# A two-block transformer kernel: 96 of 512 tokens of the expert stage taken out of the dense products and computed from fetched rows

## The reference

```python
def one_block(hx):                                   # 128 tokens
    q = (hx @ w_q).reshape(TOKEN_BLOCK, PEER_HEADS, 2, PEER_HALF)
    s = jnp.einsum('nhpd,hpkd->nhpk', q, sub_keys).astype(jnp.float32)
    top_s, top_i = lax.top_k(s, PEER_TOPK)
    ...                                              # best 16 of the 16 x 16 sums, for 8 heads
    expert = (i1 * N_KEYS + i2).reshape(TOKEN_BLOCK, PEER_HEADS * PEER_TOPK)
    gate = jax.nn.softmax(best_s, axis=-1).reshape(TOKEN_BLOCK, PEER_HEADS * PEER_TOPK)
    act = jax.nn.gelu(jnp.einsum('nd,ned->ne', hx, u[expert]), approximate=False)
    return jnp.einsum('ne,ned->nd', gate * act, v[expert])
```

## Time and profile before

| | us |
|---|---|
| median of 3 runs | 2600.27 (2599.69 to 2601.42) |
| the profiled execution, whole | 2599.47 |
| its span, first to last instruction | 2597.4 |
| TensorE busy | 2467.7 |
| POOL busy | 1556.1 |
| VectorE busy | 1379.4 |
| ScalarE busy | 594.9 |
| mean granted TensorE clock | 0.981 |

### The profile page before, as it was taken

How to read it: one execution, slowest core, us unless ns; L and a number is a source line. 1 busy time by engine, 2 the same in 40 slices (tenths; PEclk the granted TensorE clock), 3 DMA queues, 4 the chain that set the end, 5 groups by cost and what they waited for, 6 DMA issues and landing times. The chain is left out here.

```text
span 2597.4 us, 37806 instructions
## 1 busy us (share of the span) xinstructions
PE 2467.7 (95%) x12856; PEld 1258.9 (48%) x12856; DVE 1379.4 (53%) x2401; ACT 594.9 (23%) x1238; POOL 1556.1 (60%) x1048
## 2 busy tenths in 40 slices
PE   6979989999999999989999999999899898999997
PEld 3435534444555555434444444444357544457743
DVE  6695748999677777129722222240204533554434
ACT  2313211111222222111111111110216332245412
POOL 6763459888776676799866666660570067830063
PEclk8989999999999999999999999999999899999999
DMA  6324443555457857877755656560220022310021
GB/s 262 104 73 162 143 149 125 155 150 153 135 154 240 253 157 237 266 258 265 243 203 201 205 199 207 198 217 17 82 98 1 9 82 94 101 49 1 9 73 49
DMA packets 189246, 375.31 MB, mean 144 GB/s; under 512 B 13664, under 2 KB 79200, under 8 KB 189152
## 3 DMA queue, kind: packets, MB, share of 16 engines
q1 hardware_dynamic: 119696, 332.54, 38.3%
q10 hardware_dynamic: 69456, 41.50, 5.4%
HBM read 302.68 MB, written 71.30 MB: 144 GB/s over the span
## 5 line engine op out<-in xcount | busy, mean ns | idle before, releaser
L687 PE MATMUL ps<-hT,parts 128*128 128x512 f16 x4800 | 1057.3, 381 | 38.1 <-DVE arena L1397 14.5
L636 POOL TENSOR_SCALAR parts<-ring 128x1024 f16<-128x1024 f32 x261 | 289.3, 1108 | 806.7 <-PE ps L687 781.2
L687 PEld LDWEIGHTS ps<-hT,parts 128*128 128x128 f16 x4800 | 467.2, 98 | 599.2 <-issue 23.4
L687 PE MATMUL ps<-arena 128*128 128x512 f16 x3072 | 668.7, 381 | 6.8 <-DVE arena L1738 6.8
L639 POOL TENSOR_TENSOR parts<-ring,parts 128x1024 f16<-128x1024 f32 x261 | 566.6, 2171 | 21.8
L687 PEld LDWEIGHTS ps<-arena 128*128 128x128 f16 x3072 | 301.5, 98 | 374.9 <-issue 16.8
L1733 DVE TENSOR_TENSOR arena<-arena 128x512 f32<-128x512 f32 x128 | 142.3, 1112 | 438.2 <-DMA arena<-gate_mem 435.2
L657 POOL TENSOR_TENSOR arena<-ring,arena 128x1024 f16<-128x1024 f32 x128 | 283.2, 2213 | 10.6
L637 POOL TENSOR_SCALAR ring<-ring 128x1024 f32<-128x1024 f32 x261 | 281.0, 1077 | 0.0
L655 POOL TENSOR_SCALAR arena<-ring 128x1024 f16<-128x1024 f32 x128 | 147.6, 1153 | 171.6 <-PE ps L687 171.6
L1228 ACT ACTIVATE spare<-ps 128x512 f32<-128x512 f32 x128 | 76.5, 597 | 567.5 <-PE ps L687 421.2
(11 more groups left out here) (171 smaller groups left out, 2257.5 us busy)
## 6 DMA issues: line engine op xcount, KB each, us to landing
ring<-w SPq DMA_DIRECT2D x133, 512.0 KB, 3.3
ring<-u SPq DMA_DIRECT2D x128, 512.0 KB, 3.9
ring<-v SPq DMA_DIRECT2D x128, 512.0 KB, 3.4
act_mem<-spare SPq DMA_DIRECT2D x128, 256.0 KB, 4.0
gate_mem<-arena ACTq DMA_DIRECT2D x4, 8192.0 KB, 43.0
arena<-act_mem SPq DMA_DIRECT2D x128, 256.0 KB, 3.6
arena<-gate_mem SPq DMA_DIRECT2D x128, 256.0 KB, 3.8
arena<-ada_w SPq DMA_DIRECT2D x48, 512.0 KB, 5.6
```

Source lines behind the costliest of these rows:

```text
L636: G.tensor_scalar(dst[:, 0, :], src, WS, 1.0, ALU.mult, ALU.mult).then_inc(scaled, 1)
L687: ins = [T.matmul(out_, a, b, start=start and j == 0, stop=stop and j == 2) for j, (a, b) in enumerate(((lhs[0], rhs[0]), (lhs[0], rhs[1]) ...
```

## The change

The last 96 tokens leave the dense products. All widths of 512 columns in both halves become 416 (`DENSE`), 52 groups of gates are built instead of 64, in batches of 104 tokens (pieces of 416 bytes), and `act_mem` and `gate_mem` shrink to 416 columns.

For the 96 tokens VectorE makes row numbers from the chosen experts; ScalarE's queue stores them and the gates to `pick_mem` and loads them back, so that each of the 128 partitions holds one token and a quarter of its experts: 3 sets of 32 tokens, 32 picks each, 96 fetches of 128 rows. POOL fetches each with an indirect DMA, 128 rows of 4 KB, one per partition, into 6 buffers (`ROWS_AHEAD`); a fetch waits until VectorE has used the row block six before. In the up half TensorE turns the 96 tokens of `hT` into token rows in the accumulator (`turn_few`, 64 small matmuls per set), and VectorE makes 96 products with sum over 1024 features, after its last pick. The first 6 fetches stand after tile 55, the others before the tiles 104 to 127, four each. In the down half VectorE adds each fetched v row, times its weight, to a sum of its set (`add_few`); these fetches stand between the v tiles, some 0.86 per chunk; 24 small matmuls at the end add the four quarters of each token.

The work of cutting moves too: for tiles 104 to 127, and for the high half of all v tiles, ScalarE makes the passes that scale or copy (`raise_tile`, `v_tile_high`) and POOL only subtracts. SyncE's loads run 5 tiles ahead of stores and pairs instead of 8. TensorE waits for all 96 dots before the down half and for all 96 row sums before its end.

The diff, cut to its core:

```diff
-BATCH = 128
+SET = 32
+SETS = 3
+FEW = SET * SETS
+DENSE = S - FEW
+BATCH = DENSE // 4
+GROUPS = DENSE // GROUP
+SIDES = P // SET
+ROWS_AHEAD = 6
+PER_TILE = 4
+U_LEAD, V_LEAD = 5, 5
 ZG, ZG_HEAD = 10, 5
 AT_EXPS, AT_TURN, AT_GATES = 40, 44, 48
+FETCH = AT_GATES + GROUP
+RAISED = AT_GATES + GROUPS + RING
...
+        ROOM = 2 * CHUNKS * P - ROWS_AHEAD * D
+        arena = sb("arena", [P, ROOM + ROWS_AHEAD * D])
+        fetched_rows = arena[:, ROOM:ROOM + ROWS_AHEAD * D].rearrange("p (a b) -> p a b", a=ROWS_AHEAD)
+        few_idx, few_gate, few_dot = (root[:, j * FEW:(j + 1) * FEW] for j in range(3))
+        fold = root[:, 3 * FEW:3 * FEW + SET]
...
+        w_parts = cut.parts(2 * GROUP, DENSE)
+        pair = cut(4, 2, DENSE)
+        prod = c_row[:, 0:2 * DENSE].rearrange("p (a b) -> p a b", a=2)
...
+        def few_rows(j):
+            b = (4, 6, 2)[j]
+            return ps[:, b:b + 2, :].rearrange("p a b -> p (a b)")
+        def fetch_chunk(k):
+            return 112 * k // FEW
...
-                sp.dma_start(tile_of(act_mem, c), gelu[:, r % 2, :]).then_inc(act_out[r % 2], 16)
...
-            for c in range(GROUP):
+                sp.dma_start(tile_of(act_mem, c), gelu[:, r % 2, 0:DENSE]).then_inc(act_out[r % 2], 16)
+            for c in range(U_LEAD):
                 load(T_EXP + c, u_in[c])
-            with sp.Fori(0, (CHUNKS - GROUP) // RING) as it:
+            with sp.Fori(0, TAIL // RING) as it:
                 for r in range(RING):
                     c = it * RING + r
-                    load(T_EXP + GROUP + r, tile_of(u_in, c + GROUP), it)
+                    load(T_EXP + U_LEAD + r, tile_of(u_in, c + U_LEAD), it)
                     store_act(r, c)
...
             for c in range(TAIL, CHUNKS):
-                load(S_V + c - TAIL, v_in[c - TAIL])
+                n = c + U_LEAD
+                if n < CHUNKS:
+                    load(T_EXP + n, u_in[n])
+                elif n < CHUNKS + RING:
+                    load(S_V + n - CHUNKS, v_in[n - CHUNKS])
                 store_act(c, c)
...
                 sp.wait_ge(act_out[i], 16 * CHUNKS // 2)
-            for c in range(4):
-                load(S_V + GROUP + c, v_in[GROUP + c])
-            with sp.Fori(1, (CHUNKS - GROUP) // 4) as it:
+            for c in range(RING, RING + V_LEAD):
+                load(S_V + c, v_in[c])
+            with sp.Fori(1, TAIL // 4) as it:
                 for r in range(4):
-                    load(S_V + GROUP + r, tile_of(v_in, it * 4 + (GROUP + r)), it)
+                    load(S_V + V_LEAD + r, tile_of(v_in, it * 4 + (V_LEAD + r)), it)
                     load_pair(r, it * 4 + r, False)
-            for c in range(CHUNKS - GROUP, CHUNKS):
+            for c in range(TAIL, CHUNKS):
+                if c + V_LEAD < CHUNKS:
+                    load(S_V + c + V_LEAD, v_in[c + V_LEAD])
                 load_pair(c, c, False)
...
-                pool.wait_ge(scaled, it * 2 * RING + 2 * (n + 1))
+                pool.wait_ge(scaled, it * 2 * RING + 2 * (n + 1 - raised_by_act))
                 G.tensor_tensor(dst[:, 1, :], src, dst[:, 0, :], ALU.subtract).then_inc(parts_ready, 1)
...
+            def cut_raised(n):
+                pool.wait_ge(raised, 2 * (n - T_EXP - RAISED + 1))
+                src, dst = ring[:, n % RING, :], parts[:, n % RING, :, :]
+                G.tensor_tensor(dst[:, 1, :], src, dst[:, 0, :], ALU.subtract).then_inc(parts_ready, 1)
+            def fetch(n):
+                if n >= ROWS_AHEAD:
+                    wait_apart(rows_used, n - ROWS_AHEAD + 1)
+                rows = u_rows_in if n < FEW else v_in.rearrange("c p n -> (c p) n")
+                at = n % FEW
+                G.indirect_dma_start(
+                    out=fetched_rows[:, n % ROWS_AHEAD, :], out_offset=None, in_=rows,
+                    in_offset=bass.IndirectOffsetOnAxis(ap=few_idx[:, at:at + 1].bitcast(U32), axis=0),
+                ).then_inc(rows_fetched[n % ROWS_AHEAD], 16)
...
-            def cut_v(c, it=0):
-                if c >= 2 * GROUP:
-                    pool.wait_ge(down, it * 2 * GROUP + (c - 2 * GROUP + 1))
-                wait_apart(loaded[(S_V + c) % RING], it * 64 + 16 * ((S_V + c) // RING + 1))
...
+            def cut_v(c):
+                pool.wait_ge(v_high, c + 1)
                 src, dst = ring[:, (S_V + c) % RING, :], v_parts[:, c % (2 * GROUP), :, :]
-                G.tensor_scalar(dst[:, 0, :], src, 1.0, 1.0, ALU.mult, ALU.mult).then_inc(v_high, 1)
-                pool.wait_ge(v_high, it * 2 * GROUP + (c + 1))
                 G.tensor_tensor(dst[:, 1, :], src, dst[:, 0, :], ALU.subtract).then_inc(parts_ready, 1)
             for n in range(RING):
                 cut_tile(n, n)
-            cut_tiles(RING, T_TWO, 0)
-            for i in range(2):
-                pool.wait_ge(gates_out[i], 16 * (S // BATCH) // 2)
-            for c in range(2 * GROUP):
+            cut_tiles(RING, T_EXP + FETCH, 0)
+            pool.wait_ge(pick_loaded, 16 * 2 * SIDES)
+            for n in range(ROWS_AHEAD):
+                fetch(n)
+            cut_tiles(T_EXP + FETCH, T_EXP + RAISED, 0)
+            n = ROWS_AHEAD
+            for c in range(RAISED, CHUNKS):
+                for _ in range(PER_TILE):
+                    if n < FEW:
+                        fetch(n)
+                        n += 1
+                cut_raised(T_EXP + c)
+            while n < FEW + ROWS_AHEAD:
+                fetch(n)
+                n += 1
+            for c in range(CHUNKS):
+                while n < 2 * FEW and fetch_chunk(n - FEW) <= c:
+                    fetch(n)
+                    n += 1
                 cut_v(c)
-            with pool.Fori(0, CHUNKS // (2 * GROUP) - 1) as it:
-                for c in range(2 * GROUP, 4 * GROUP):
-                    cut_v(c, it)
-            cut_tiles(T_TWO, T_END, CHUNKS)
+            cut_tiles(T_TWO, T_END, CHUNKS, CHUNKS - RAISED)
...
-                    first, last = three(ps[:, r % 2, :], piece(T_EXP + r, k * P, P), hr(k), k == 0, k == KC - 1)
+                    hi, lo = hr(k)
+                    first, last = three(ps[:, r % 2, 0:DENSE], piece(T_EXP + r, k * P, P),
+                                        (hi[:, 0:DENSE], lo[:, 0:DENSE]), k == 0, k == KC - 1)
...
-            ups(AT_GATES + 4, AT_GATES + S // GROUP, 4)
-            ups(AT_GATES + S // GROUP, CHUNKS)
+            ups(AT_GATES + 4, AT_GATES + GROUPS, 4)
+            def turn_few(j):
+                first = DENSE + j * SET
+                for k in range(KC):
+                    for side in range(SIDES):
+                        for h, half in enumerate(hr(k)):
+                            mm = T.matmul(few_rows(j)[side * SET:(side + 1) * SET, k * P:(k + 1) * P],
+                                          half[:, first:first + SET], ident_h, start=(h == 0), stop=(h == 1))
+                mm.then_inc(few_turned, 1)
+            for j in range(min(SETS, 2)):
+                turn_few(j)
+            ups(AT_GATES + GROUPS, AT_GATES + GROUPS + 4)
+            if SETS == 3:
+                pe.wait_ge(gates, 2 * GROUPS)
+                turn_few(2)
+            ups(AT_GATES + GROUPS + 4, CHUNKS)
...
+            pe.wait_ge(gates, 2 * GROUPS)
+            pe.wait_ge(rows_used, FEW)
...
-                    first, last = three(ps[:, o, :], lhs, rhs, isinstance(c, int) and c == 0, False)
...
+            pe.wait_ge(rows_used, 2 * FEW)
...
-                    first, last = three(ps[:, o, :], lhs, rhs, False, c == CHUNKS - 1)
-                last.then_inc(down, 1)
+                    three(ps[:, o, 0:DENSE], lhs, rhs, False, c == CHUNKS - 1)
+                for j in range(SETS):
+                    at = DENSE + j * SET
+                    mm = T.matmul(ps[:, o, at:at + SET], few_sum(j)[:, o * P:(o + 1) * P], fold, start=True, stop=True)
+                mm.then_inc(down, 1)
...
+                A.activation(gelu[:, r % 2, 0:DENSE], ps[:, r % 2, 0:DENSE], ACT.Gelu, scale=1.0 / WS).then_inc(gelu_ready, 1)
...
-            gelus(AT_EXPS, AT_GATES)
+            gelus(AT_EXPS, AT_TURN)
+            act.wait_ge(pick_ready, 1)
+            act.dma_start(pick_mem[0], pick_row[P - FEW:P, :]).then_inc(pick_stored, 16)
+            act.dma_start(pick_mem[1], chosen[P - FEW:P, NT - 1, 2, :]).then_inc(pick_stored, 16)
+            gelus(AT_TURN, AT_GATES)
+            act.wait_ge(pick_stored, 32)
+            for j, dst in enumerate((few_idx, few_gate)):
+                for q in range(SIDES):
+                    rows = pick_mem[j][:, q * SET:(q + 1) * SET].rearrange("(s t) k -> t s k", s=SETS)
+                    act.dma_start(dst[q * SET:(q + 1) * SET, :].rearrange("p (s k) -> p s k", s=SETS),
+                                  rows).then_inc(pick_loaded, 16)
             per = BATCH // GROUP
...
+            for b in range(DENSE // BATCH):
...
+            def raise_tile(n):
+                act.wait_ge(loaded[n % RING], 16 * (n // RING + 1))
```

(67 more changed lines are left out.)

72 lines of the change are left out of this document (44 added, 28 removed).

## The result

The changed kernel takes 2473.3 us (2472.65 to 2474.53, 4 runs) against 2599.98 for the kernel before on the same chip: a ratio of 0.9514, 95% interval 0.9498 to 0.953. Its profiled execution took 2473.4 us, span 2471.6.

What follows compares the result with a forecast made beforehand. TensorE, busy 95% of the span, was taken to bound the kernel. Up half and down start -12 and down half -103 made -115 from 2599.47: 2484, or 2485 against the median; range 2445 to 2590.

Steps and rivals of the forecast that it cites:

- Chunks 0 to 99: Up half before the rows: TensorE idles 24 us for routing, first gates at 666.9, then 5.10 us a group until 928.
- The turn of the 96 tokens: Start of the row phase: two turns, 128 small matmuls priced like the gates' small products, 7.1 us.
- The row phase: End of up half: DMA sets 1.9 us a fetch, 171 us plus 10 for the last gate store; gives back 42.
- R1: Rival, row phase and down half: POOL's fetch price sets both, 2639 at 2.1 us, over 2600 from about 1.9; chance 0.13.
- Start of the down half: Between the halves: TensorE waits 8 us for ScalarE's five v passes, a high and a low part; down begins at 1134.
- Down half: All 128 down chunks: 4.35 us each, bounds 4.21 and 5.0, in total 573 us against 676, so -103.
- the loop: Down half: pair loads wait behind v load, POOL's cut, ScalarE's v pass and an earlier high part; 3.4 us a chunk.
- the stretching: Down half: VectorE and POOL slow each other reading SBUF together; they need 3.6 us a chunk, under TensorE's 4.21.
- R2: Rival, down half: the new loop and VectorE and POOL stretching each other hold it at 4.7 a chunk, 2530; chance 0.20.
- R3: Rival, row phase and down half: all overlaps, fetches at 1.70 and down chunks at 4.21, 2449; chance 0.14.
- R5: Rival, matmuls: no gain because a narrower product is no shorter, 2620; chance 0.01.
- R4: Rival, gate stores: 416-byte pieces cost double, 86 us for 43, giving 2515; sign: stores well above 43; chance 0.09.

Runs made afterwards that it cites:

- run 12: Changed kernel with exponentials, turn and first gates at chunks 48, 52, 56 instead of 40, 44, 48, and six row fetches per tile: 2470.56 us.
- run 4: Changed kernel with each u row fetched and used to half its width only, the other half of those products left out: 2458.88 us (two runs).
- run 3: Changed kernel with GpSimd again cutting tiles 104 to 127 alone, in three passes instead of one subtraction: 2511.43 us.
- run 8: Changed kernel with SyncE issuing the first four pairs' loads after the last activation store, not before that of chunk 125: 2479.89 us.
- run 9: Changed kernel with SyncE issuing the loads of v tiles 4 to 8 ahead of its wait for the last activation stores: 2476.23 us.
- run 11: Changed kernel with tile loads and v passes four ahead instead of five, and first six v rows fetched singly behind the first v subtractions: 2472.14 us.
- Run 7: Changed kernel with ScalarE making four v passes, not five, before the first high part and staying four ahead; loads still five ahead: 2480.48 us.
- run 5: Changed kernel with four row buffers instead of six: 2832.76 us.
- run 1: Changed kernel with GpSimd instead of ScalarE making the high half of each v tile again: 2592.9 us.
- run 2: Changed kernel with GpSimd making the v tiles' high half again and VectorE's row sums cut to 32 of 1024 columns: 2534.23 us.
- run 6: Changed kernel with tile loads and ScalarE's v passes four ahead instead of five: 2464.7 us.

## Why the prediction was right, and where its terms were off

The forecast was 2485, the time is 2473.3, and the mechanism is the one forecast: the up half gives little, the down half the gain.

*Chunks 0 to 99.* Right: 28.9 us of stop, the turn over at 643.77 (643.6), first gates at 665.3 (666.9), 5.11 a chunk (5.10). Taking the stop out won 2.7 us in the median, within the runs' spread (run 12).

*The turn of the 96 tokens.* Mis-sized: 2.0 us where I had 7.1 from the gates' small matmuls.

*The row phase.* The pace was right, 1.93 for 1.9, and so was GpSimd's fetch, 1.25 us for 1.2, which takes R1's condition away. It ended at 1113 instead of 1126: it began 8 us earlier and took 5 less. That the pace fits is in part luck. The 1.9 stood for rows, tiles and activation stores, with 10 us on top for the rest of the last gate store. But that store lay in the row stretch with all its 16400 packets, which took 15.6% of the DMA engines' time from 927 to 1100, 27 us, and the measured 1.93 carries it. Without it the DMA engines would have come to some 1.64 a row, an estimate from these shares, and GpSimd's 1.79 (run 4) would have been the bound. Runs 3 and 4 show that DMA and GpSimd are 7% apart: the second bound was nearer than "hidden" suggests.

*Start of the down half.* The step that was furthest off: 22.4 us where I had 8. I counted ScalarE's passes (1.04 us each, 1.1 forecast) and left out what they wait for, a store's landing and the fifth v tile's, both asked for beside six row fetches on full DMA engines. Taking the first of these waits away lengthened the second (run 8), asking for the tile 2.4 us earlier didn't bring it earlier (run 9), and a start 11 us earlier brings the last read forward by 3 us (run 11).

*Down half.* 553.3 for 573. Neither the loop nor the stretching cost the 0.14 a chunk that I had put in: TensorE's 4.21 stands, so R2 didn't come. But both are real and close. Run 7 shows the loop with the v passes one nearer, run 5 another one through the row buffers, runs 1 and 2 the stretching with one pass more. My 3.6 us for VectorE and GpSimd together was too low: in run 6, where VectorE hardly waits, it makes a chunk in 4.0, only 5% under TensorE's 4.21. So the margin was 0.2 us a chunk and not 0.6, and at the end of the down half it was 4.9 us in all, a bound that the prediction didn't name. With GpSimd's high pass added it was 5.26: by the same working, that is 3.18 + 2.3 less 0.8, I'd have had 4.6, too low again.
The Trainium skill ("SBUF — State Buffer", Who interferes with whom) has the two block each other fully, which for that run makes 5.5: nearer than my working. In the run with short sums it makes 4.4 against 4.71, since the sum leaves out GpSimd's own fetches. For run 6 the prediction's 4.40 by that rule is as far above 4.0 as its 3.6 is below.

*R3* was half right, the down half at 4.21 and the rows not. *R5* is out with 4.21 us a chunk. *R4* is out: the first three stores of 416-byte pieces landed in 43.4 to 43.7 us, those of 512-byte pieces in 42.8 to 43.4 with as many pieces. In these stores the price went by piece, not by byte. R4's sign, a store well above 43 us, did come, in the last store's 170.9. It isn't R4's doing: the store shared full engines with the row fetches, and its pieces took 27 us of the engines' time, less than the 31 to 32 of each of the first three.
The Trainium skill ("DMA: Bandwidth & Descriptors", Specifications) has read-modify-write below 512 bytes; the trace shows 31 to 32 us of the engines' time for 416-byte pieces where as many of 512 took 29, and 27 in the last store, so an added cost, if any, is small here.

The sum against the forecast: start +4, down half -20, after it +5, together -11. The +5, behind the last read, has no cause that a run shows; without it the sum would have been off by 16.

## What to carry to other kernels

When the busiest engine's work shrinks by a fifth, list the time of every other engine and of the DMA engines in each stretch, undisturbed and disturbed, and expect the next bound within a few per cent: one pass of 1 us on the wrong engine was worth 120 us here, on an engine that was only 60% busy before. Where a queue is served in order, count how far each engine may run ahead of the other before buffers are taken away or loads moved earlier; four ahead was no worse than five here, and left VectorE more in hand. Where the busiest engine must see all of another's work before its last part, as before the last eight chunks here, that other engine's end is a bound of its own: look for it in the timeline. At a seam where the DMA engines are full, asking for one thing earlier or later moved the wait, and brought the end forward by 3 us at most.

## What the runs showed of the hardware

- A matmul with outputs of 32 partitions and 128 columns, written to four groups of 32 partitions in turn, took 1.98/128 us = 15.5 ns, where one with 128 partitions and 128 columns takes 1.06/16 = 66 ns.
- An indirect DMA of 128 pieces of 4 KB costs GpSimd 0.94 us undisturbed, 1.25 from one to the next, and in the down half 1.12 in the median, up to 1.76.
- With six such fetches in flight beside the tile loads, one lands in 8.4 us at 403 GB/s from 930 to 1120; with four in 6.4 us at 359.
- 6656 KB in 416-byte pieces took 43.7 us in the median, 8192 KB in 512-byte pieces 43.0: the same time per piece. Beside the row fetches the same 6656 KB took 170.9 us.
- Beside each other, VectorE's and GpSimd's work takes longer. From 1200 to 1600, GpSimd's subtraction, 2.13 us alone, took 2.31 in the mean in the changed kernel, 2.46 in run 6 and 2.87 in run 1; VectorE's product of a pair, 0.59 alone, took 1.38, 1.25 and 2.31.
